# An encoder layer on one core: another order at the entries of gate/up and of down, other slots, some low parts on GpSimd

## The chip, the cores and the metric

One core of one Trainium2 chip runs the kernel. The time is in device microseconds (us). Engines: PE is TensorE, DVE is VectorE, ACT is ScalarE, POOL is GpSimd, SP is SyncE, which only issues DMAs here. SBUF is the on-chip memory, PSUM the accumulators of TensorE, eight banks of 128x512 float32.

## The reference

```python
u = rms_norm(x, norm_mix_g)
proj = einsum('bsd,de->bse', u, w_in)            # q k v | b c h
att  = diff_attention(...) ; conv = bg * short_conv(cg * hv, conv_w)
x = x + einsum('bse,ed->bsd', concat(att, conv), w_out)
z = rms_norm(x, norm_ffn_g)
hid = silu(z @ w_gate) * (z @ w_up)              # 1024 -> 2816
x = x + hid @ w_down
return rms_norm(x, final_g)
```

Everything is float32, the sequence has 2048 rows of 1024. The change concerns the way from the projection with w_out (the rows `x + mixed @ w_out`) through gate/up to the start of down.

## The kernel before, in words

**Three products for one.** TensorE multiplies in a format with fewer bits. Each operand is split: ACT makes the high part (`*_hi`), DVE the low part (`*_lo = raw - hi`), and TensorE makes hi*hi + hi*lo + lo*hi.

**Projection and tiles of z.** 16 tiles of 128 rows (`N_ROWS`, in the order `ORDER`) go one after another: PE projects (`project_tile`, into PSUM banks 0-1 for even and 2-3 for odd tiles, `o_sums`), DVE adds the rows (`add_rows`), ACT squares (`square_rows`), DVE makes the mean, POOL the power -1/2 (`rsqrt_row`), DVE scales to `z_tile` (`norm_rows`), PE turns it (`turn_z`, into banks 4 to 7), ACT evacuates it into `zt` (`evacuate_z`). SP stores the rows (`store_rows`). For each pair of tiles DVE forms four differences `zt_sum` (`sum_z`), and SP stores zt and zt_sum as seven blocks (`store_z`, seven DMAs of 256 KB) into `z_dram`. `evacuate_z` of a pair's first tile waits until the pair before is stored.

**Gate/up as seven products.** The product z @ [gate, up] is made as a 2x2 block product with seven instead of eight block products (k = 0 to 6), for 22 chunks of 128 columns (steps) and for two halves of 1024 rows: 44 steps. Each block product is 4 x 3 matmuls of 128x512. Its operands are the block z_k (`z_slot`, 128x4x512, hi and lo, loaded once in a half) and the weights w_k (`w_slot`, made anew in each step; `sum_weights` forms the sums). Products share four banks (`c_bank`, `BANK_OF`), so in a step product 2 waits for `p_0` (ACT's copy of bank 0), product 5 for `make_u_3`, product 6 for `make_c_22` on DVE. `silu_first`, `hidden` and `silu_second` make the hidden block, which SP stores (`store_hid`).

**Where z blocks come from.** In half 0 blocks 0 to 3 go through `z_stage` (SP loads, ACT's and DVE's `split_z`), blocks 4 to 6 are loaded straight into the place of their low part (`split_placed_z`). In half 1 all seven go through three stages (`load_z_next`): a stage is loaded again once the low part made from it is done. They are made during the last step of half 0 (`later`), each after that step's product k has released its slot.

**Down.** For each of 4 groups of 512 rows, 22 chunks: SP loads 128x512 of the hidden block and 128x1024 of w_down (`load_down`) into one of two slots, ACT and DVE split (`split_down`), PE multiplies into eight banks (`down_chunk`, 24 matmuls). A slot is loaded again once its low parts are done. Ahead of chunk 2 SP issues the y rows and the gain of the end.

**What sets the order.** Every engine runs its instructions in the order of the code, with hand-written semaphores. Only the waits listed in the code hold an instruction up, and everything behind it on that engine with it; SP's DMAs too are issued in one order.

## Time and profile before

| | |
|---|---|
| median of 3 runs (2779.66 to 2782.27) | 2781.87 us |
| the profiled execution: its own time | 2779.97 us |
| its span | 2778.1 us |
| PE busy | 2665.7 us, 96% of the span, 12280 matmuls |
| DVE / ACT / POOL busy | 54% / 37% / 18% |
| granted clock of TensorE over the span | 0.988 |
| lines of gate/up (L1734) on the chain that ended last | 15% |
| lines of down (L1792) on that chain | 17% |

The span is the part of the execution that the profile covers; 1.9 us lie outside it. The profile lists for each group of instructions its busy time and the idle time of its engine just ahead of it, with what ended that. An engine's idle time costs only where the end of the kernel hangs on it. A matmul of 128x512 is shown with 390 ns but one begins every 227 ns; durations of matmuls overlap.

### The profile page before, as it was taken

The page shows a single profiled execution, that of the slowest core. Times are in us where ns is not written, and L with a number is a line of the kernel's source. Part 1 is how long each engine was busy: PE and PEld are TensorE (multiplying, and loading weights), DVE is VectorE, ACT ScalarE, POOL GpSimd, SP SyncE. Part 2 cuts the span into 40 slices and gives each one's busy share as a digit, 9 for nine tenths or more (in the row PEclk, how much of TensorE's full clock was granted, in tenths as well). Part 3 has the DMA queues.
Part 4 walks back from the last instruction along what each step waited for, and adds up shares of the span by engine and source line. Part 5 has one row for each costly group of instructions (what it writes and reads, how often), then busy time and mean ns, then how long its engine had stood idle before and what let it go on. Part 6 is the DMA issues. An engine that isn't in the chain of part 4 may idle for free. (4 is left out here: it accounts for less than half of the span.)

```text
span 2778.1 us, 34594 instructions
## 1 busy us (share of the span) xinstructions
PE 2665.7 (96%) x12280; PEld 2184.4 (79%) x12280; DVE 1511.9 (54%) x2203; ACT 1021.9 (37%) x1429; POOL 501.2 (18%) x343
## 2 busy tenths in 40 slices
PE   7999999979999999989989999989999999999997
PEld 5788888857777777778868888878888878888886
DVE  5311122258878887854466666676666643434343
ACT  5210000047667676742243333343333323323232
POOL 1000000047777777720000000000000000000000
PEclk9999999999999999999989999999999999999999
DMA  5542111223131221047762222252222235556563
GB/s 171 147 124 87 57 38 38 61 64 71 28 75 46 68 57 31 20 157 224 229 219 76 83 91 72 87 174 91 72 87 88 75 120 152 170 175 207 146 203 116
DMA packets 257359, 298.29 MB, mean 107 GB/s; under 512 B 15200, under 2 KB 175456, under 8 KB 257280
## 3 DMA queue, kind: packets, MB, share of 16 engines
q1 hardware_dynamic: 254400, 287.83, 35.1%
q0 software_dynamic: 2304, 8.39, 0.7%
q8 instruction: 46, 0.75, 0.1%
q10 hardware_dynamic: 576, 1.05, 0.1%
q14 instruction: 33, 0.27, 0.0%
HBM read 212.28 MB, written 84.93 MB: 107 GB/s over the span
## 5 line engine op out<-in xcount | busy, mean ns | idle before, releaser
L1734 PE MATMUL banks<-z_hi,w_hi 128*128 128x512 f32 x1204 | 469.9, 390 | 8.4 <-ACT p L947 5.5
L1734 PE MATMUL banks<-z_hi,w_lo 128*128 128x512 f32 x1204 | 469.4, 390 | 0.0
L1734 PE MATMUL banks<-z_lo,w_hi 128*128 128x512 f32 x1204 | 469.3, 390 | 0.0
L1546 PE MATMUL projected<-u_t_hi,w_part_hi 128*128 128x512 f32 (+1 forms) x768 | 300.3, 391 | 5.3 <-DVE u_t_lo L1090 2.6
L1546 PE MATMUL projected<-u_t_lo,w_part_hi 128*128 128x512 f32 (+1 forms) x768 | 299.3, 390 | 0.0
L1546 PE MATMUL projected<-u_t_hi,w_part_lo 128*128 128x512 f32 (+1 forms) x768 | 299.3, 390 | 0.0
L697 POOL TENSOR_TENSOR exp<-exp,exp 128x2048 f32<-128x2048 f32 x64 | 295.6, 4618 | 5.3
L1734 PEld LDWEIGHTS banks<-z_hi,w_hi 128*128 128x128 f32 x1204 | 226.8, 188 | 56.8 <-issue 5.9
L1734 PEld LDWEIGHTS banks<-z_lo,w_hi 128*128 128x128 f32 x1204 | 226.8, 188 | 47.0
L1734 PEld LDWEIGHTS banks<-z_hi,w_lo 128*128 128x128 f32 x1204 | 226.6, 188 | 47.2
L842 ACT ACTIVATE exp<-exp,neg_max 128x2048 f32<-128x2048 f32 x128 | 257.3, 2010 | 15.3 <-DVE neg_max L1228 14.4
L726 POOL TENSOR_TENSOR y_rstd<-y_mean,neg_half 128x1 f32<-128x1 f32 x16 | 8.7, 546 | 1343.4 <-DVE y_mean L1496 1343.4
L943 ACT ACTIVATE w_hi<-w_sum 128x512 fp32r<-128x512 f32 x176 | 111.3, 633 | 319.1 <-PE banks L1734 307.3
L1792 PE MATMUL banks<-down_hi,hid_hi 128*128 128x512 f32 x704 | 217.7, 391 | 3.9 <-DVE down_lo L1484 3.9
L1792 PE MATMUL banks<-down_lo,hid_hi 128*128 128x512 f32 x704 | 217.7, 390 | 0.0
L1792 PE MATMUL banks<-down_hi,hid_lo 128*128 128x512 f32 x704 | 217.4, 390 | 0.0
L852 ACT ACTIVATE a_t_hi<-tile_turned 128x512 fp32r<-128x512 f32 x256 | 148.7, 601 | 158.1 <-PE tile_turned L1622 157.8
L1240 DVE TENSOR_TENSOR a_t_lo<-tile_turned,a_t_hi 128x512 fp32r<-128x512 f32 x256 | 172.1, 687 | 54.3 <-ACT a_t_hi L852 54.2
L1604 PE MATMUL scores<-k_sum,q_part_hi 128*128 128x512 f32 x512 | 179.4, 432 | 18.7 <-DVE half_min L1228 10.3
L1481 DVE TENSOR_TENSOR hid_lo<-hid_raw,hid_hi 128x512 fp32r<-128x512 f32 x88 | 60.9, 693 | 247.6 <-ACT hid_hi L1029 247.6
L1228 DVE CUSTOM_DVE_ANT_0 exp<-scores,window,half_min 128x1024 f32<-128x1024 f32 x128 | 163.9, 1280 | 31.7 <-PE scores L1604 26.1
L1029 ACT ACTIVATE hid_hi<-hid_raw 128x512 fp32r<-128x512 f32 x88 | 55.6, 632 | 324.2 <-PE banks L1792 313.4
(143 smaller groups left out, 4420.9 us busy)
## 6 DMA issues: line engine op xcount, KB each, us to landing
down_raw<-in_w_down SPq DMA_DIRECT2D x88, 512.0 KB, 4.4
gate_raw<-in_w_gate SPq DMA_DIRECT2D x44, 512.0 KB, 4.7
up_raw<-in_w_up SPq DMA_DIRECT2D x44, 512.0 KB, 5.6
hidden_t<-hid_stage SPq DMA_DIRECT2D x88, 256.0 KB, 2.7
hid_raw<-hidden_t SPq DMA_DIRECT2D x88, 256.0 KB, 3.7
w_raw<-in_w_in SPq DMA_DIRECT2D x24, 512.0 KB, 5.3
projected_t<-stage SPq DMA_DIRECT2D x48, 256.0 KB, 2.5
z_stage<-z_blocks SPq DMA_DIRECT2D x11, 1024.0 KB, 5.8
```

What stands on the lines that cost most here:

```text
L697: nc.gpsimd.tensor_tensor(exp_0[:, slot_0], exp_0[:, slot_0], exp_1[:, slot_1], ALU.add).then_inc(mixed_ready, 1)
L842: nc.scalar.activation(rows, rows, ACT.Exp, scale=-1.0, bias=neg_max[:, t % 2, part:part + 1], accum_out=exp_sum[:, part, t % 16:t % 16 + ...
L852: nc.scalar.activation(dst, turned_bank(h, t, index), ACT.Copy).then_inc(group_hi, 1)
L943: nc.scalar.activation(w_slot[k][0][:, :, :], src, ACT.Copy).then_inc(w_hi_ready_2, 1)
L1029: nc.scalar.activation(hid_part[slot][0][:, :], hid_raw[:, slot], ACT.Copy).then_inc(f_hi_ready, 1)
L1228: nc.vector.tensor_tensor_reduce(out=rows[:, half * HALF:(half + 1) * HALF], in0=scores[:, unit % 2], in1=window[:, window_slice(t, half)] ...
L1240: nc.vector.tensor_tensor(parts[1][at], turned_bank(h, t, index), parts[0][at].bitcast(FP32), ALU.subtract).then_inc(group_lo, 1)
L1481: nc.vector.tensor_tensor(hid_part[slot][1][:, :], hid_raw[:, slot], hid_part[slot][0][:, :].bitcast(FP32), ALU.subtract).then_inc(f_lo_re ...
L1546: last = nc.tensor.matmul(projected[:, bank * BANK:(bank + 1) * BANK], w_part[w][:, r, kt], u_t[u][:, kt, rows], start=(kt == 0 and n == 0 ...
L1604: last = nc.tensor.matmul(scores[:, unit % 2, b * BANK:(b + 1) * BANK], q_part[n][:, (t // 4) % 2, part, t % 4 * P:(t % 4 + 1) * P], k_sum ...
L1734: last = nc.tensor.matmul(c_bank[BANK_OF[k]], w_slot[k][w][:, kt], z_slot[k][z][:, kt], start=(kt == 0 and t == 0 and k in (0, 1, 3, 4)), ...
L1792: last = nc.tensor.matmul(y_banks[j][:, c * BANK:(c + 1) * BANK], hid_part[slot][h][:, j * P:(j + 1) * P], down_part[slot][w][:, c * BANK: ...
```

## The change

- The outputs of a step (`up_0`, `silu_0`, `hid_stage`), the weight slots 5 and 6, stage 1 of z and `hid_raw` change places in SBUF. The new place of weight slots 5 and 6 is free when the projection has ended, no longer when the rows have been stored.
- `c_bank` are now banks 0 to 3 (before 0, 1, 4, 5), so that product 3 waits for the last addition of rows instead of an evacuation. `y_banks` follow.
- SP: `store_z` of pair 6 moves behind the loads of z blocks 4 to 6 and the rows of the last tile. The loads for half 1 no longer wait for the stores of the rows, and wait for low parts on their engine.
- ACT: z_hi 3 stands ahead of the square of the last tile; the weights 3 to 6 follow, then z_hi 4, 5 and 6 with the two last evacuations between them.
- DVE: no `sum_z` of pairs 6 and 7, low part of z block 3 ahead of the last mean; the low part of block 5 goes away.
- POOL: makes `sum_z` of pairs 6 and 7 and the low parts of block 5 (half 0) and of blocks 1, 3 and 5 (half 1), with a semaphore of its own (`z_lo_pool`).
- Down: ACT splits chunk 1 ahead of `silu_second`, DVE splits chunk 0 ahead of `make_c_12`.

ScalarE at the entry of gate/up, before (`z_hi_100` is block 3, `z_hi_102`, `_104`, `_106` are blocks 4 to 6, `w_hi_139` to `_145` the weights 3 to 6):

```order
L921 ACTIVATE zt<-banks 128x1024
L914 ACTIVATE z_tile,row_sumsq<-rows 128x1024
L921 ACTIVATE zt<-banks 128x1024
L928 ACTIVATE z_hi_100<-z_stage_147 128x2048
L943 ACTIVATE w_hi_139<-w_sum 128x512
L947 ACTIVATE p_150<-banks 128x512
L943 ACTIVATE w_hi_141<-w_sum 128x512
L921 ACTIVATE zt<-banks 128x1024
L943 ACTIVATE w_hi_143<-up_raw_159 128x512
L943 ACTIVATE w_hi_145<-w_sum 128x512
L932 ACTIVATE z_hi_102<-z_lo_103 128x2048
L932 ACTIVATE z_hi_104<-z_lo_105 128x2048
```

and now:

```order
L965 ACTIVATE zt<-banks 128x1024
L972 ACTIVATE z_hi_100<-z_stage_147 128x2048
L958 ACTIVATE z_tile,row_sumsq<-rows 128x1024
L991 ACTIVATE p_150<-banks 128x512
L987 ACTIVATE w_hi_139<-w_sum 128x512
L987 ACTIVATE w_hi_141<-w_sum 128x512
L987 ACTIVATE w_hi_143<-up_raw_159 128x512
L987 ACTIVATE w_hi_145<-w_sum 128x512
L976 ACTIVATE z_hi_102<-z_lo_103 128x2048
L965 ACTIVATE zt<-banks 128x1024
L976 ACTIVATE z_hi_104<-z_lo_105 128x2048
L965 ACTIVATE zt<-banks 128x1024
```

The last tile's square moved behind z_hi 3, both evacuations (`zt<-banks`) behind the weights and between the placed blocks.

SyncE there, before and now:

```order
L581 DMA z_stage_147<-z_blocks 128x4x512
L533 DMA z_blocks<-zt 128x4x128 x3
L536 DMA z_blocks<-zt_sum 128x4x128 x4
L527 DMA rows_x<-rows 128x1024
L571 DMA z_lo_103<-z_blocks 128x4x512
L571 DMA z_lo_105<-z_blocks 128x4x512
L571 DMA z_lo_107<-z_blocks 128x4x512
L527 DMA rows_x<-rows 128x1024
```

```order
L540 DMA rows_x<-rows 128x1024
L584 DMA z_lo_103<-z_blocks 128x4x512
L584 DMA z_lo_105<-z_blocks 128x4x512
L584 DMA z_lo_107<-z_blocks 128x4x512
L540 DMA rows_x<-rows 128x1024
L546 DMA z_blocks<-zt 128x4x128 x3
L549 DMA z_blocks<-zt_sum 128x4x128 x4
```

The seven stores of a pair moved behind the three loads and the rows.

GpSimd from the last power op of the projection to the change of the half, now (before, the power op was its last instruction there; `z_lo_105` is block 5, `z_lo_97` and `z_lo_101` are blocks 1 and 3 of the second half):

```order
L734 TENSOR_TENSOR row_rstd<-row_mean,neg_half 128x1
L751 TENSOR_TENSOR z_lo_105<-z_lo_105,z_hi_104 128x2048
L741 TENSOR_TENSOR zt_sum<-zt 128x512
L742 TENSOR_TENSOR zt_sum<-zt 128x512
L744 TENSOR_TENSOR zt_sum<-zt,zt_sum 128x512
L746 TENSOR_TENSOR zt_sum<-zt,zt_sum 128x512
L751 TENSOR_TENSOR z_lo_97<-z_stage_148,z_hi_96 128x2048
L751 TENSOR_TENSOR z_lo_101<-z_stage_147,z_hi_100 128x2048
L751 TENSOR_TENSOR z_lo_105<-z_stage_149,z_hi_104 128x2048
```

Four low parts are new on this engine, and eight differences, of which four stand ahead of the power op.

VectorE at the change of the half, before (`z_lo_95` is block 0, `z_lo_97` block 1, `z_lo_99` block 2; `u_151<-banks` is the addition after product 1, `u_152` the one that product 5 waits for) and now:

```order
L1314 TENSOR_TENSOR z_lo_95<-z_stage_147,z_hi_94 128x2048
L1360 TENSOR_TENSOR u_151<-banks,p_150 128x512
L1354 TENSOR_TENSOR w_lo_136<-w_sum,w_hi_135 128x512
L1347 TENSOR_TENSOR w_sum<-gate_raw_157,up_raw_159 128x512
L1349 TENSOR_TENSOR w_sum<-gate_raw_157,w_sum 128x512
L1314 TENSOR_TENSOR z_lo_97<-z_stage_148,z_hi_96 128x2048
L1354 TENSOR_TENSOR w_lo_138<-gate_raw_157,w_hi_137 128x512
L1314 TENSOR_TENSOR z_lo_99<-z_stage_149,z_hi_98 128x2048
L1360 TENSOR_TENSOR u_152<-banks,u_151 128x512
L1354 TENSOR_TENSOR w_lo_140<-w_sum,w_hi_139 128x512
```

```order
L1355 TENSOR_TENSOR z_lo_95<-z_stage_147,z_hi_94 128x2048
L1401 TENSOR_TENSOR u_151<-banks,p_150 128x512
L1395 TENSOR_TENSOR w_lo_136<-w_sum,w_hi_135 128x512
L1388 TENSOR_TENSOR w_sum<-gate_raw_157,up_raw_159 128x512
L1390 TENSOR_TENSOR w_sum<-gate_raw_157,w_sum 128x512
L1395 TENSOR_TENSOR w_lo_138<-gate_raw_157,w_hi_137 128x512
L1355 TENSOR_TENSOR z_lo_99<-z_stage_149,z_hi_98 128x2048
L1401 TENSOR_TENSOR u_152<-banks,u_151 128x512
L1395 TENSOR_TENSOR w_lo_140<-w_sum,w_hi_139 128x512
```

z_lo 1 is gone from between the sums and the weights 2; z_lo 3 and z_lo 5 go likewise further on.

The diff (unchanged lines cut):

```diff
@@ -269,22 +269,22 @@
-        w_at = ((147456, 149504), (204288, 206336), (208384, 194048), (167936, 169984), (172032, 174080), (40960, 43008), (45056, 47104))
+        w_at = ((147456, 149504), (204288, 206336), (208384, 194048), (167936, 169984), (172032, 174080), (196096, 198144), (200192, 202240))
         w_slot = [[at(w_at[k][n], f"w_{'hi' if n == 0 else 'lo'}_{k}", [P, 4, P], F32R) for n in range(2)] for k in range(7)]
-        z_stage = [at(offset, f"z_stage_{i}", [P, 4, BANK]) for i, offset in enumerate((131072, 196096, 73728))]
+        z_stage = [at(offset, f"z_stage_{i}", [P, 4, BANK]) for i, offset in enumerate((131072, 65536, 73728))]
         p_0 = at(32768, "p_0", [P, BANK])
...
         up_1 = at(38912, "up_1", [P, BANK])
-        up_0 = at(65536, "up_0", [P, BANK])
-        silu_0 = at(67584, "silu_0", [P, BANK])
-        hid_stage = at(69632, "hid_stage", [P, 2, BANK])
+        up_0 = at(40960, "up_0", [P, BANK])
+        silu_0 = at(43008, "silu_0", [P, BANK])
+        hid_stage = at(45056, "hid_stage", [P, 2, BANK])
         g_raw = [at(81920, "gate_raw_0", [P, KT, P]), at(139264, "gate_raw_1", [P, KT, P])]
...
         down_raw = at(73728, "down_raw", [P, 2, D])
-        hid_raw = at(196096, "hid_raw", [P, 2, BANK])
+        hid_raw = at(65536, "hid_raw", [P, 2, BANK])
         hid_part = [[at(16384 * s + 2048 * n, f"hid_{'hi' if n == 0 else 'lo'}_{s}", [P, BANK], F32R) for n in range(2)] for s in range(2)]
@@ -303,9 +303,9 @@
         z_turned = [banks[:, 4 + 2 * n:6 + 2 * n].rearrange("p b (k q) -> p (b k) q", q=P) for n in range(2)]
-        c_bank = [banks[:, b] for b in (0, 1, 4, 5)]
+        c_bank = [banks[:, b] for b in range(4)]
         BANK_OF = (0, 1, 0, 2, 3, 2, 3)
-        y_banks = [banks[:, b:b + 2].rearrange("p b n -> p (b n)") for b in (2, 6, 0, 4)]
+        y_banks = [banks[:, b:b + 2].rearrange("p b n -> p (b n)") for b in (4, 6, 0, 2)]
@@ -314,6 +314,19 @@
+        Z_ON_POOL = ((5,), (1, 3, 5))
...
+        def z_count(half, k, on_pool):
...
+            return sum((j in Z_ON_POOL[n]) == on_pool for n in range(half + 1) for j in range(7 if n < half else k + 1))
...
+        def wait_z(engine, half, k):
+            if k in Z_ON_POOL[half]:
+                engine.wait_ge(z_lo_pool, z_count(half, k, True))
+            else:
+                engine.wait_ge(z_lo_ready, z_count(half, k, False))
@@ -328,7 +341,7 @@
         z_loaded = [sem(f"z_loaded_{i}") for i in range(3)]
-        z_hi_ready, z_lo_ready = sem("z_hi_ready"), sem("z_lo_ready")
+        z_hi_ready, z_lo_ready, z_lo_pool = sem("z_hi_ready"), sem("z_lo_ready"), sem("z_lo_pool")
         z_placed = [sem(f"z_placed_{k}") for k in (4, 5, 6)]
@@ -562,7 +575,7 @@
                     load_gate_up(0, 0)
-                if n % 2 == 0 and n >= 2:
+                if n % 2 == 0 and 2 <= n < N_ROWS - 2:
                     store_z(n // 2 - 1)
@@ -570,6 +583,8 @@
                 store_rows(n)
+                if n == N_ROWS - 1:
+                    store_z(N_ROWS // 2 - 2)
                 if n + 2 < N_ROWS:
@@ -577,7 +592,7 @@
                     else:
-                        sp.wait_ge(z_lo_ready, n - 10)
+                        wait_z(sp, 0, n - 11)
                     sp.dma_start(z_stage[0][:, :, :], z_dram[0, n - 10].rearrange("k p t -> p k t")).then_inc(z_loaded[0], 16)
@@ -588,9 +603,11 @@
-                sp.wait_ge(z_lo_ready, 7 + k - 2)
+                if k >= 3:
+                    wait_z(sp, 1, k - 3)
+                elif k == 0:
+                    wait_z(sp, 0, 3)
                 sp.wait_ge(z_stored[1], 16 * 28)
-                sp.wait_ge(rows_stored[k % 2], 16 * (N_ROWS // 2))
                 sp.dma_start(z_stage[k % 3][:, :, :], z_dram[1, k].rearrange("k p t -> p k t")).then_inc(z_loaded[k % 3], 16)
@@ -643,7 +660,8 @@
             sp.wait_ge(hid_stored[1], 16 + 16 * F_CHUNKS)
-            sp.wait_ge(z_lo_ready, 14)
+            wait_z(sp, 1, 5)
+            wait_z(sp, 1, 6)
             load_down(0, 0, 0, False)
@@ -715,8 +733,34 @@
-            for n in range(N_ROWS):
+            def sum_z(pair):
+                pool.wait_ge(zt_ready, 2 * pair + 2)
+                pool.wait_ge(z_stored[(pair - 1) // 4], 16 * 7 * ((pair - 1) % 4 + 1))
+                b11, b21, b12, b22 = zt[:, 0, 0:4], zt[:, 0, 4:8], zt[:, 1, 0:4], zt[:, 1, 4:8]
+                t1, t2, t3, t4 = (zt_sum[:, n] for n in range(4))
+                nc.gpsimd.tensor_tensor(t1, b12, b11, ALU.subtract).then_inc(zt_sum_ready, 1)
+                nc.gpsimd.tensor_tensor(t3, b22, b12, ALU.subtract).then_inc(zt_sum_ready, 1)
+                pool.wait_ge(zt_sum_ready, 4 * pair + 1)
+                nc.gpsimd.tensor_tensor(t2, b22, t1, ALU.subtract).then_inc(zt_sum_ready, 1)
+                pool.wait_ge(zt_sum_ready, 4 * pair + 3)
+                nc.gpsimd.tensor_tensor(t4, b21, t2, ALU.subtract).then_inc(zt_sum_ready, 1)
...
+            def split_z(half, k):
+                pool.wait_ge(z_hi_ready, 7 * half + k + 1)
+                raw = z_stage[k % 3][:, :, :] if half else z_slot[k][1][:, :, :].bitcast(FP32)
+                nc.gpsimd.tensor_tensor(z_slot[k][1][:, :, :], raw, z_slot[k][0][:, :, :].bitcast(FP32), ALU.subtract).then_inc(z_lo_pool, 1)
...
+            for n in range(N_ROWS - 1):
                 rsqrt_row(n)
+            sum_z(N_ROWS // 2 - 2)
+            rsqrt_row(N_ROWS - 1)
+            for k in Z_ON_POOL[0]:
+                split_z(0, k)
+            sum_z(N_ROWS // 2 - 1)
...
+            for k in Z_ON_POOL[1]:
+                split_z(1, k)
@@ -977,10 +1021,14 @@
             for n in range(N_ROWS):
+                if n == N_ROWS - 1:
...
+                    act.wait_ge(o_summed, N_ROWS)
+                    split_z(0, 3, 0, 4)
                 square_rows(n)
...
                     split_m(n + 2)
-                if n >= 1:
+                if 1 <= n < N_ROWS - 1:
                     evacuate_z(n - 1)
@@ -988,26 +1036,20 @@
-            act.wait_ge(o_summed, N_ROWS)
-            split_z(0, 3, 0, 4)
-            split_w(0, 0, 3, True)
             copy_p_0(0)
-            split_w(0, 0, 4, True)
+            for k in range(3, 7):
+                split_w(0, 0, k, True)
+            split_placed_z(4)
+            evacuate_z(N_ROWS - 2)
+            split_placed_z(5)
             evacuate_z(N_ROWS - 1)
+            split_placed_z(6)
...
             act.wait_ge(rows_stored[1], 16 * (N_ROWS // 2))
-            for k in range(5, 7):
-                split_w(0, 0, k, True)
-            split_placed_z(4)
-            split_placed_z(5)
+            silu_first(0)
             split_w(1, 1, 0)
             split_w(1, 1, 1)
-            split_placed_z(6)
...
-            act.wait_ge(z_stored[1], 16 * 28)
-            silu_first(0)
             for k in range(2, 7):
@@ -1038,9 +1080,8 @@
             split_down(0, 0, 0, False)
+            split_down(0, 1, 1, False)
             silu_second(STEPS - 1)
-            act.wait_ge(product_ready, 7 * STEPS)
-            split_down(0, 1, 1, False)
             for group in range(4):
@@ -1427,8 +1468,10 @@
                     dve.wait_ge(ffn_gain_loaded, 16)
+                if n == N_ROWS - 1:
+                    split_z(0, 3, 0)
                 norm_rows(n)
-                if n % 2 == 0 and n >= 2:
+                if n % 2 == 0 and 2 <= n < N_ROWS - 2:
                     sum_z(n // 2 - 1)
@@ -1438,24 +1481,23 @@
                     split_z(0, n - 11, 0)
-            split_z(0, 3, 0)
+            make_u_2(0)
             split_w(0, 0, 3)
-            make_u_2(0)
-            for k in range(4, 7):
-                split_w(0, 0, k)
+            split_w(0, 0, 4)
             split_placed_z(4)
-            sum_z(N_ROWS // 2 - 1)
+            split_w(0, 0, 5)
             make_u_3(0)
-            split_placed_z(5)
+            split_w(0, 0, 6)
+            split_placed_z(6)
+            make_c_22(0)
             sum_weights(1, 1, 0)
             split_w(1, 1, 0)
-            make_c_22(0)
             split_w(1, 1, 1)
-            split_placed_z(6)
             sum_weights(1, 1, 1)
...
-            dve.wait_ge(z_stored[1], 16 * 28)
+            dve.wait_ge(rows_stored[0], 16 * (N_ROWS // 2))
+            dve.wait_ge(rows_stored[1], 16 * (N_ROWS // 2))
             make_c_21(0)
@@ -1468,7 +1510,7 @@
                 gate_up_step(2 * pair + 2, 0)
-            gate_up_step(F_CHUNKS - 1, 1, lambda k: split_z(1, k, k % 3))
+            gate_up_step(F_CHUNKS - 1, 1, lambda k: None if k in Z_ON_POOL[1] else split_z(1, k, k % 3))
             with dve.Fori(F_CHUNKS // 2, F_CHUNKS - 1) as pair:
@@ -1506,9 +1548,9 @@
             hidden(STEPS - 1, 0)
+            split_down(0, 0, 0)
             make_c_12(STEPS - 1)
             hidden(STEPS - 1, 1)
-            split_down(0, 0, 0)
             split_down(0, 1, 1)
@@ -1713,7 +1755,7 @@
                 if fresh is not None:
-                    pe.wait_ge(z_lo_ready, 7 * fresh + k + 1)
+                    wait_z(pe, fresh, k)
@@ -1738,7 +1780,7 @@
                 pe.wait_ge(w_lo_ready_2, k + 1)
-                pe.wait_ge(z_lo_ready, k + 1)
+                wait_z(pe, 0, k)
                 if k == 2:
@@ -1766,7 +1808,7 @@
             first_product(2)
-            pe.wait_ge(zt_ready, N_ROWS - 1)
+            pe.wait_ge(rows_added, N_ROWS)
             for k in range(3, 7):
```

## Rows read from the trace of the kernel before

**Rows 1.** timeline of TensorE: start, us, engine, line, operation [idle before <- releaser].

```profile
1416.73 0.77 PE L1750 MATMUL banks<-z_hi,w_hi 128*128 128x512 f32 x1 [2.57 <-ACT p L947]
...
1430.47 0.77 PE L1750 MATMUL banks<-z_hi,w_hi 128*128 128x512 f32 x1 [5.27 <-DVE z_lo L1320]
...
1441.96 0.47 PE L1750 MATMUL banks<-z_hi,w_hi 128*128 128x512 f32 x1 [2.99 <-issue]
...
1446.31 0.47 PE L1734 MATMUL banks<-z_hi,w_hi 128*128 128x512 f32 x1
...
1843.43 0.50 PE L1734 MATMUL banks<-z_hi,w_hi 128*128 128x512 f32 x1 [2.47 <-DVE u L1360]
...
1860.82 0.77 PE L1734 MATMUL banks<-z_hi,w_hi 128*128 128x512 f32 x1 [5.51 <-ACT p L947]
...
2281.02 1.22 PE L1792 MATMUL banks<-down_hi,hid_hi 128*128 128x512 f32 x2 [3.91 <-DVE down_lo L1484]
```

**Rows 2.** windows, TensorE alone: stretch, us, busy (instructions), granted clock, DMA share, GB/s.

```profile
1600.00:1800.00 200.00, 200.00 (x884) 1.00 0.28 85
1416.73:1425.04 8.31, 8.31 (x24) 0.65 1.05 351
1860.82:1866.08 5.26, 5.26 (x12) 0.50 0.15 55
```

**Rows 3.** timeline of DVE and of GpSimd in the first stage.

```profile
33.09 1.27 DVE L1084 SCALAR_TENSOR_TENSOR u_tile<-x_tile,rstd,mix_gain 128x1024 f32<-128x1024 f32 x1
33.26 1.52 POOL L682 TENSOR_TENSOR rstd<-mean_eps,neg_half 128x1 f32<-128x1 f32 x1 [0.69 <-DVE mean_eps L1077]
...
40.58 0.69 DVE L1096 TENSOR_TENSOR stage<-projected,stage 128x512 fp32r<-128x512 f32 x1
40.73 0.55 POOL L682 TENSOR_TENSOR rstd<-mean_eps,neg_half 128x1 f32<-128x1 f32 x1 [5.95 <-DVE mean_eps L1077]
```

**Rows 4.** single lines: durations in ns, least/median/most, first and last start, shapes.

```profile
L697 POOL TENSOR_TENSOR exp<-exp,exp x64: 4507/4627/4651, 588.6 to 1194.4; 128x2048 f32<-128x2048 f32 x64
...
L1314 DVE TENSOR_TENSOR z_lo<-z_stage,z_hi x3: 2287/2292/2292, 1384.4 to 1415.6; 128x2048 fp32r<-128x2048 f32 x3
```

**Rows 5.** DMA issues in windows at 1401.6, 1411.7 and 1418.0: KB, us to landing.

```profile
z_stage<-z_blocks SPq DMA_DIRECT2D x1, 1024.0 KB, 5.5
...
z_lo<-z_blocks SPq DMA_DIRECT2D x1, 1024.0 KB, 11.4
...
z_blocks<-zt SPq DMA_DIRECT2D x1, 256.0 KB, 10.0
```

**Rows 6.** timeline of SP and ScalarE at the entry of gate/up.

```profile
1409.86 2.57 SPq L571 DMA_DIRECT2D z_lo<-z_blocks  x3
...
1412.76 1.03 ACT L921 ACTIVATE zt<-banks 128x1024 f32<-128x1024 f32 x1 [1.88 <-DMA z_blocks<-zt_sum]
```

**Rows 7.** timeline of ScalarE, DVE and SP at the change of the half.

```profile
1833.46 1.91 ACT L928 ACTIVATE z_hi<-z_stage 128x2048 fp32r<-128x2048 f32 x1
...
1835.28 0.68 DVE L1360 TENSOR_TENSOR u<-banks,p 128x512 f32<-128x512 f32 x1
...
1850.33 0.69 DVE L1386 TENSOR_TENSOR hid_stage<-up,silu 128x512 f32<-128x512 f32 x1
...
1851.51 0.37 SPq L594 DMA_DIRECT2D z_stage<-z_blocks  x1
...
1857.77 1.91 ACT L928 ACTIVATE z_hi<-z_stage 128x2048 fp32r<-128x2048 f32 x1 [7.16 <-DMA z_stage<-z_blocks]
```

**Rows 8.** timeline of SP, ScalarE and TensorE at the entry of down, chunk 2.

```profile
2282.49 0.41 SPq L640 DMA_DIRECT2D hid_raw<-hidden_t  x1
...
2290.73 0.63 ACT L1029 ACTIVATE hid_hi<-hid_raw 128x512 fp32r<-128x512 f32 x1 [10.75 <-DMA hid_raw<-hidden_t]
2291.94 1.06 ACT L1031 ACTIVATE down_hi<-down_raw 128x1024 fp32r<-128x1024 f32 x1 [0.58 <-DMA down_raw<-in_w_down]
...
2294.41 0.64 PE L1792 MATMUL banks<-down_hi,hid_hi 128*128 128x512 f32 x2
```

## The prediction

> **What bounds the kernel now.** Read the waits of TensorE first, because TensorE is busy for 96% of the span and the steady loops leave it no idle time: what a change outside its instruction count can give is only where it stands still or runs at its low clock. The waits that belong to the lines of this change are four kinds, and the timeline puts them in three places [rows 1]:
>
> - *Entry of gate/up, 1412 to 1446.3 us.* Products 2 to 6 of step 0 stand behind an evacuation (2.57), the low part of z block 4 (5.27) and that of block 6 (2.99).
> - *Change of the half, 1831 to 1866 us.* Product 5 waits 2.47, product 2 of the next step 5.51.
> - *Entry of down, 2277 to 2294 us.* The first chunk waits 3.91.
>
> Together about 23 us. Each wait also costs clock. In the steady loop 884 matmuls take 200 us, 0.226 each, so a product of 12 takes 2.7; after the 5.51 us wait the granted clock was 0.50 (the 1.2 GHz level) and 12 matmuls took 5.26 us; after the 2.57 us wait 24 of them took 8.31 us instead of 5.4 [rows 2]. So an idle time of 2.6 us or more brings some 2.6 us with it, one of 2.47 brought none. At the entry of gate/up three such stretches bring about 7 us. In all some 35 us of 2780 could go, if nothing else set these places. So the question at each place is what comes last once the named wait is gone.
>
> **Two things the sum needs.** *DVE and GpSimd exclude each other.* GpSimd's tiny power op takes 0.55 us, also beside a DVE instruction that reads PSUM (started 40.73, beside the one of 40.58). The one started at 33.26 took 1.52: a DVE instruction with two SBUF inputs had begun at 33.09 and ended at 34.36 [rows 3]. Three of the 16 power ops of that line met such a DVE instruction, and exactly these three took 1.5 us. I take it that the exclusion holds in the other direction too; the rows don't show that, since in attention, where GpSimd works long, DVE's instructions all read PSUM. GpSimd's add of 128x2048 took 4.62 us, DVE's low part of the same shape 2.29 [rows 4]; a quarter of the first, 1.2 us, is my estimate for 128x512.
> The Trainium skill, page "SBUF — State Buffer", section "SBUF: two separate sides", says the same in both directions: GpSimd and a DVE instruction with two SBUF inputs share a port pair as "an exclusive lock, not a bandwidth split". By it the loser stands for the whole instruction. It speaks against this change: moving work to GpSimd then frees next to nothing on DVE.
> *The DMA queue lands in order at some 350 GB/s.* The third 1 MB block, issued at 1411.7, landed after 11.4 us; a 256 KB store issued at 1418.0 behind it took 10.0 us; the fourth z_stage block, issued at 1401.6, landed at 1407.1 [rows 5]. Between 1416.7 and 1425.0 the queue moved 351 GB/s [rows 2].
>
> **Part 1, entry of gate/up.** Removed: the late issue of the three blocks (before from 1409.86 on, behind the stores of pair 6 [rows 6]; now at 1406.0, when the last projection ends), ScalarE's wait for the row stores ahead of the weights 5 and 6, DVE's 2 x 4 sums (4 x 0.6 us each), one low part on DVE. The last tile's chain: its addition on DVE comes at 1406.1 instead of 1408.5. But z_hi 3 now stands ahead of its square on ScalarE (1407.2 to 1409.1), then the low part z_lo 3 on DVE ahead of the mean; with GpSimd's four sums between, z_lo 3 runs 1409.7 to 1412.0, the last sum to 1413.2, the power op to 1413.8, z_tile to 1415.1. The turn comes 2 us later than before, product 2 starts at about 1416, product 4 ends at about 1427: before, only products 2 and 3 were done by 1425.
> What comes last next: ScalarE evacuates tile 14 into zt only once pair 6 is stored. Before, that wait ended at 1412.76 [rows 6]. Now pair 6 is issued behind everything: left in the queue at 1407.1 are the rows of tile 14 (0.52 MB), the three blocks (3.15), the rows of tile 15 (0.52), pair 6 (1.84), 6.03 MB at 351 GB/s = 17.2 us, so it lands at 1424.5. And in ScalarE's order z_hi 5 stands behind that evacuation: evacuation to 1426, z_hi 5 to 1427.9, evacuation of tile 15 to 1428.8, z_hi 6 to 1430.7. GpSimd makes z_lo 5 in 4.6 us, to 1432.6. Product 5 starts there, 5.6 us after product 4 ended, at the low clock (5.3 us), product 6 follows and ends at 1440.7. DVE's z_lo 6 waits for GpSimd and is done by 1434.9, the sum for product 6 by 1435.5, the first weights of step 1 by 1440.5 even if GpSimd's second group of sums comes between each pair: in time. Step 1 began at 1446.3 [rows 1]: **-5.5 us**, from -10 (pair 6 lands at 1420) to -1 (a full queue that holds up SP).
>
> **Part 2, change of the half.** Low parts 1, 3 and 5 go from DVE to GpSimd; the loads' issues keep their order. Before: z_hi 1 starts at 1833.46 and ends at 1835.3, DVE adds from PSUM at 1835.28 [rows 7]. Now GpSimd begins z_lo 1 at 1835.4, while DVE does that addition, and holds until 1840.0. DVE's next instruction (the low weights, two SBUF inputs) ends at 1840.7 instead of 1836.6; two sums, low weights and z_lo 2 to 1844.7; the addition that product 5 needs ends at 1845.4, and TensorE has waited 4.4 us instead of 2.5, with the low clock behind it. GpSimd takes z_lo 3 from 1844.8 to 1849.4: DVE's low weights 3 wait for it and with them the addition for product 6 (1850.7; product 5 ends then too). z_lo 4 on DVE ends at 1853.5, z_hi 5 is ready at 1853.2 (product 5 must have ended), GpSimd gets in with z_lo 5 while DVE adds from PSUM, to 1858.2. The hidden block, before at 1850.33, comes to 1858.2; SP's load of z block 6 stands behind its store (before 1851.51), is issued at 1859.5 instead, lands 6 us later, z_hi 6 ends at 1867.3 instead of 1859.7 [rows 7]. Behind it on ScalarE is p_0, for which TensorE waited 5.51 us. **+7 us**; if DVE gets its hidden block in before GpSimd +4; from +3 to +9 under exclusion. Where both run side by side: z_lo 4 still waits for its load (lands at 1845.4), the hidden block comes at 1850.1, the load at 1851.2: -0.3 us, at best -2.
>
> **Part 3, entry of down.** Chunk 0's low parts now go ahead of the last combination. DVE ends them at 2277.6, TensorE starts at 2277.8 instead of 2281.0, without the wait and at full clock, so chunks 0 and 1 (48 matmuls) are done at 2288.7 instead of 2294.4. But chunk 2 was just in time: its data are issued at 2282.49 behind 2.6 MB of y rows and gain, ScalarE's hid_hi waited for them until 2290.73 and down_hi until 2291.94, DVE's low part (1.2 us) filled the rest, TensorE went on at 2294.41 [rows 8]. None of these issues moves forward; SP's second store of the hidden block is 0.4 us later. So TensorE now waits 6 us at 2288.7 and starts chunk 2 at 2294.8, at the low clock (2.5 us more for the first 12 matmuls). In the kernel before, that price lay inside the time in which chunk 2 was awaited anyway. **+2.9 us**, from 0 (clock stays) to +3.5.
>
> Sum: -5.5 + 7.0 + 2.9 = **+4.4 us** on the profiled execution's 2779.97 (span 2778.1, 1.9 outside it), which is 1.9 below the median 2781.87; against the median that is 2786.3. The rest (banks, slots) changes no count and no size: 12280 matmuls before and now.
>
> **The rivals.**
> *Side by side.* GpSimd doesn't hold up DVE. For: no row shows GpSimd delaying DVE, and 4.6 us adds ran in attention without DVE's instructions there growing longer. Against: the three long power ops [rows 3]. Then -5.5 - 0.3 + 2.9 = -2.9: 2779.0.
> *The waits go as named.* Pair 6 lands early, chunk 2's data come with the chunk, no low clock: part 1 -10, part 2 -1, part 3 -3, -14 in all, 2768. For: the store of pair 6 needs only the time of its own 1.84 MB where the queue ahead is short. Against: 4 MB stand ahead of it now, and the rows of chunk 2 leave no slack [rows 5, 8].
> *Slower beyond doubt.* Exclusion as in part 2, where z_lo 5 gets ahead of the hidden block (+7.6), and pair 6 landing 4 us later, which takes part 1 to -1.5: -1.5 + 7.6 + 2.9 = +9, 2791. It decides as soon as pair 6 lands after 1428.
> *The change does less than it says:* GpSimd's sums come so late that store and load of the next weights stall step 1; a loss of 2 to 4 us more in part 1, inside the case above.
>
> **How the numbers follow.** Exclusion with part 1 near -5.5: 0.52, 2786.3 (own range 2781 to 2789). Exclusion with a late queue: 0.18, 2791. Side by side: 0.18, 2779. Waits go as named: 0.12, 2768. A measurement can tell about 0.2%, 5.6 us: faster is under 2776.3, slower over 2787.4. Faster: all of the last, a third of side by side, a little of the first: 0.20. Slower: most of the late-queue case, a third of the first: 0.33. The range 2773 to 2792 leaves out the last rival and the tails.
>
> **What would show it.** Part 1: ScalarE's zt of tile 14 waits for a store until about 1424, TensorE idles before product 5 and not before product 4. Part 2: DVE instructions that took 0.69 are shown with 2 to 5 us beside z_lo on GpSimd, z block 6 is issued near 1859. Part 3: TensorE starts down at 2278 (on the clock of before) and stands 6 us before chunk 2. I am wrong if DVE's durations stay at 0.69 beside GpSimd, if pair 6 lands by 1420, or if chunk 2's hid_raw lands before 2289.

## The result and the profile after

| | median | range, runs |
|---|---|---|
| kernel before | 2778.41 us | 2775.04 to 2782.27, 18 |
| changed kernel | 2782.48 us | 2780.08 to 2786.30, 18 |

The ratio is 1.0019 with a 95% interval of 1.0012 to 1.0025: 3 to 7 us slower, a small loss but clear of no change. Forecast were +4.4 us over the kernel before, or 2786.3 us by the 2781.87 us that the kernel before had then; its median of 18 runs is 3.5 us lower, and the changed kernel's 2782.48 us lies 3.8 under the forecast time. The profiled execution has a span of 2782.4 us, against 2778.1 before; the counts of matmuls are equal.

*A measure that is free of the front.* What lies ahead of gate/up varies by some us between executions, for every kernel here: in the thirteen profiles the 15th addition of rows on DVE starts between 1398.0 and 1404.7 us. So the stages are measured from the start of that addition. Its row in the trace after, then TensorE's first product line of the steps from 1 on (how many, shortest/mean/longest in ns, first to last start):

```profile
1399.50 1.22 DVE L1344 TENSOR_TENSOR rows<-banks,rows 128x1024 f32<-128x1024 f32 x1
L1776 PE MATMUL banks<-z_hi,w_hi x1204: 389/389/792, 1438.0 to 2277.5; 128*128 128x512 f32 x172
```

and the same two of before:

```profile
1401.50 1.22 DVE L1303 TENSOR_TENSOR rows<-banks,rows 128x1024 f32<-128x1024 f32 x1
L1734 PE MATMUL banks<-z_hi,w_hi x1204: 389/389/765, 1446.3 to 2276.3; 128*128 128x512 f32 x172
```

Three lengths follow for each kernel: from that addition to step 1 (44.8 us before, 38.5 after), from there to the last gate/up matmul (830.0, 839.5), and from that to the end of the span (501.8, 504.9). These lengths don't repeat to a tenth: among kernels with the same code in a stage (table below) they differ by 1.1 us to step 1 (37.6 to 38.7; before and e11 by 2.2), by 1.7 in the middle (837.8 to 839.5) and by 1.7 in the last (503.9 to 505.6). Of the 9.5 us that the middle one grew, 2.3 lie ahead of the change of the half (DVE's addition `u<-banks,p` comes 389.0 us after step 1 began in before, 391.3 in after), so 7.2 lie at it. The three parts of the forecast are therefore: entry of gate/up -6.3 + 2.3 = **-4.0** (forecast -5.5), change of the half **+7.2** (+7.0), entry of down **+3.1** (+2.9). The span's difference of 4.3 has 2.0 us of a shorter front in it: 1399.50 against 1401.50.

TensorE's timeline after, its first matmul behind each long wait (start, length, instruction, in brackets the idle time ahead and what ended it). The rows that answer are [rows 1]:

```profile
1412.94 1.13 PE L1751 MATMUL banks<-identity,z_tile 128*128 128x128 f32 x8 [2.26 <-DVE z_tile L1350]
1430.83 0.77 PE L1792 MATMUL banks<-z_hi,w_hi 128*128 128x512 f32 x1 [7.03 <-issue]
1445.69 0.50 PE L1776 MATMUL banks<-z_hi,w_hi 128*128 128x512 f32 x1 [1.92 <-ACT p L991]
...
1839.28 0.79 PE L1776 MATMUL banks<-z_hi,w_hi 128*128 128x512 f32 x1 [4.32 <-DVE u L1401]
1861.85 0.76 PE L1776 MATMUL banks<-z_hi,w_hi 128*128 128x512 f32 x1 [9.15 <-ACT p L991]
...
2278.92 0.74 PE L1834 MATMUL banks<-down_hi,hid_hi 128*128 128x512 f32 x2 [0.58 <-DVE down_lo L1526]
2296.20 1.22 PE L1834 MATMUL banks<-down_hi,hid_hi 128*128 128x512 f32 x2 [6.07 <-DVE down_lo L1526]
```

Three waits of the entry became one long one (product 5) and a new small one in step 1; both waits at the change of the half grew (2.47 to 4.32, 5.51 to 9.15); the 3.91 us of chunk 0 became 6.07 us ahead of chunk 2. The four long ones were followed by low clock, the one of 1.92 by the full one (granted 1.00 from 1445.69 to 1451.10). The windows behind the four (length, PE busy and count, granted clock, DMA share, GB/s):

```profile
1430.83:1436.30 5.47, 5.47 (x17) 0.68 0.16 48
1839.28:1845.00 5.72, 5.72 (x15) 0.59 0.59 183
1861.85:1867.20 5.35, 5.35 (x13) 0.50 0.15 53
2296.20:2301.60 5.40, 5.39 (x13) 0.52 0.72 210
```

*Change of the half: GpSimd, then DVE beside it.*

```profile
1829.44 4.63 POOL L751 TENSOR_TENSOR z_lo<-z_stage,z_hi 128x2048 fp32r<-128x2048 f32 x1 [390.31 <-ACT z_hi L972]
1837.84 5.21 POOL L751 TENSOR_TENSOR z_lo<-z_stage,z_hi 128x2048 fp32r<-128x2048 f32 x1 [3.77 <-ACT z_hi L972]
1847.01 4.61 POOL L751 TENSOR_TENSOR z_lo<-z_stage,z_hi 128x2048 fp32r<-128x2048 f32 x1 [3.96 <-ACT z_hi L972]
```

```profile
1829.29 0.69 DVE L1401 TENSOR_TENSOR u<-banks,p 128x512 f32<-128x512 f32 x1
1829.89 4.73 DVE L1395 TENSOR_TENSOR w_lo<-w_sum,w_hi 128x512 fp32r<-128x512 f32 x1
1834.54 0.68 DVE L1388 TENSOR_TENSOR w_sum<-gate_raw,up_raw 128x512 f32<-128x512 f32 x1
...
1836.35 2.28 DVE L1355 TENSOR_TENSOR z_lo<-z_stage,z_hi 128x2048 fp32r<-128x2048 f32 x1
...
1839.15 4.45 DVE L1395 TENSOR_TENSOR w_lo<-w_sum,w_hi 128x512 fp32r<-128x512 f32 x1
...
1847.69 4.47 DVE L1427 TENSOR_TENSOR hid_stage<-up,silu 128x512 f32<-128x512 f32 x1
```

For each instruction of GpSimd one of DVE stands with 4.5 to 4.7 us instead of 0.69, and ends some 0.55 us behind GpSimd's end (1829.44 + 4.63 = 1834.07, and DVE's 1829.89 + 4.73 = 1834.62): it began its work only then. The other direction is in GpSimd's second row: 5.21 us instead of 4.6, because DVE's z_lo 2 of 1836.35 ran until 1838.6. The addition from PSUM at 1829.29 ran with its usual 0.69 while GpSimd began. The last of them is the hidden block; behind its store stands SP's load of z block 6, and behind that ScalarE:

```profile
1852.63 0.39 SPq L611 DMA_DIRECT2D z_stage<-z_blocks  x1
```

```profile
1858.80 1.91 ACT L972 ACTIVATE z_hi<-z_stage 128x2048 fp32r<-128x2048 f32 x1 [10.86 <-DMA z_stage<-z_blocks]
```

### The profile page after: what moved, and what is told of

Same layout as the page of the kernel before. It is cut to its first block and busy times, and to the rows that moved or that the text cites. A ratio compares the mean times of both kernels' runs of the same rounds, so it can differ in the third digit from the quotient of the medians.

```text
span 2782.4 us, 34593 instructions
## 1 busy us (share of the span) xinstructions
PE 2662.5 (96%) x12280; PEld 2182.5 (78%) x12280; DVE 1514.2 (54%) x2191; ACT 1020.6 (37%) x1429; POOL 536.5 (19%) x355
```

## The experiments

Each kernel ran in five rounds with the kernel before beside it; the kernel before had 2778.53, 2777.84 and 2777.50 us in the three groups (e1, e2, e4, e5; e3, e6, e7, e8; e9 to e11). Lengths in the table are the three of above, from the profiled execution, in us. They are those of one execution: their sums and the medians differ from each other by up to 4 us (most in e5 and e11, whose profiled executions were the shortest of their runs). So a median decides what an edit is worth, and the lengths say where; a difference under 2 us between two lengths is not told from none. Why executions of one kernel differ so is open; one part that shows is the clock behind a wait (last section).

| kernel | median | ratio to before, 95% | to step 1 | step 1 to last gate/up | to the end |
|---|---|---|---|---|---|
| before | | | 44.8 | 830.0 | 501.8 |
| changed | 2782.48 | 1.0019, 1.0012 to 1.0025 | 38.5 | 839.5 | 504.9 |
| e1_half_on_vector | 2775.57 | 0.9989, 0.9980 to 0.9998 | 37.6 | 831.0 | 503.9 |
| e2_down_undone | 2780.06 | 1.0008, 0.9999 to 1.0017 | 38.4 | 837.8 | 501.7 |
| e4_y_rows_later | 2774.89 | 0.9988, 0.9979 to 0.9997 | 37.8 | 838.0 | 496.4 |
| e5_placed_first | 2776.96 | 0.9995, 0.9986 to 1.0004 | 31.0 | 838.1 | 504.1 |
| e3_block6_ahead | 2769.20 | 0.9969, 0.9958 to 0.9980 | 37.9 | 824.6 | 505.6 |
| e8_y_rows_alone | 2779.12 | 1.0008, 0.9999 to 1.0017 | 38.6 | 838.1 | 501.1 |
| e7_halves | 2779.39 | 1.0005, 0.9996 to 1.0014 | 38.7 | 836.3 | 504.5 |
| e6_all | 2754.73 | 0.9919, 0.9905 to 0.9932 | 30.9 | 824.7 | 496.7 |
| e9_block5_on_vector | 2755.36 | 0.9917, 0.9903 to 0.9931 | 33.6 | 823.5 | 496.5 |
| e10_sums_on_vector | 2755.05 | 0.9919, 0.9905 to 0.9933 | 30.8 | 823.8 | 496.4 |
| e11_before_two_places | 2766.30 | 0.9959, 0.9945 to 0.9973 | 42.6 | 822.4 | 496.1 |

### The change of the half

**e1_half_on_vector**, the changed kernel without GpSimd's low parts of the second half:

```diff
-        Z_ON_POOL = ((5,), (1, 3, 5))
+        Z_ON_POOL = ((5,), ())
```

> One part undone: the low parts 1, 3 and 5 of the second half are made by VectorE again, GpSimd keeps block 5 of the first half and the two groups of sums. Theory (GpSimd and VectorE with two SBUF inputs exclude each other, and this is what made the change of the half 7.2 us longer): the stretch from step 21 to step 23 is as in the kernel before, no VectorE instruction of 128x512 there takes over 0.7 us, z block 6 is issued some 5 us earlier; in all 7 us less than the changed kernel, -1 us against the kernel before. Rival (the stretch is longer because the stage was moved or because the loads wait for other semaphores): stays at +4 us against the kernel before.

The middle length went from 839.5 back to 831.0, the median down by 6.9 us. The moved stage and the loads' other semaphores, the rival's causes, are still in this kernel. So GpSimd's low parts alone made the loss at this place.

**e7_halves**, the changed kernel with each of GpSimd's low parts there as two instructions:

```diff
-                nc.gpsimd.tensor_tensor(z_slot[k][1][:, :, :], raw, z_slot[k][0][:, :, :].bitcast(FP32), ALU.subtract).then_inc(z_lo_pool, 1)
+                    nc.gpsimd.tensor_tensor(z_slot[k][1][:, 0:2], raw[:, 0:2], z_slot[k][0][:, 0:2].bitcast(FP32), ALU.subtract)
+                    nc.gpsimd.tensor_tensor(z_slot[k][1][:, 2:4], raw[:, 2:4], z_slot[k][0][:, 2:4].bitcast(FP32), ALU.subtract).then_inc(z_lo_pool, 1)
```

> The changed kernel with each of GpSimd's three low parts of the second half as two instructions of 128x1024 (4.6 us becomes 2.3 + 2.3). Theory (DVE waits for the GpSimd instruction that runs, and gets its turn between two): no DVE instruction there is longer than about 3.0 us (2.3 + 0.7) instead of 4.7, the hidden block comes earlier, and the change of the half costs 1 to 4 us less: about 2779 to 2781. Rival (GpSimd keeps the port as long as it has a next instruction ready): DVE's longest stay at 4.7 us and the time at 2782.5.

GpSimd's timeline and DVE's beside it, at the first of the three low parts:

```profile
1831.84 2.41 POOL L752 TENSOR_TENSOR z_lo<-z_stage,z_hi 128x1024 fp32r<-128x1024 f32 x1 [390.30 <-ACT z_hi L976]
1834.21 2.84 POOL L753 TENSOR_TENSOR z_lo<-z_stage,z_hi 128x1024 fp32r<-128x1024 f32 x1
```

```profile
1832.28 2.52 DVE L1399 TENSOR_TENSOR w_lo<-w_sum,w_hi 128x512 fp32r<-128x512 f32 x1
1834.72 2.88 DVE L1392 TENSOR_TENSOR w_sum<-gate_raw,up_raw 128x512 f32<-128x512 f32 x1
```

The two take turns, one instruction each: DVE's low weights ended 0.55 us behind GpSimd's first half (1834.80 and 1834.25), and GpSimd's second half shows 0.4 us more than its first. DVE's longest 128x512 instruction at the change of the half was 2.88 us, the kernel 3 us faster. So DVE waits for the instruction that runs, and the rival, that GpSimd keeps its place while it has a next one, fell.

**e3_block6_ahead**, e1 with the load of z block 6 ahead of the store of the hidden block:

```diff
-            for k in range(3, 6):
+            for k in range(3, 7):
                 load_z_next(k)
             store_hid(0, F_CHUNKS - 1, F_CHUNKS - 1, 0)
-            load_z_next(6)
```

> The low parts of the second half are all on DVE again, as in e1_half_on_vector, and z block 6 is loaded ahead of the store of the hidden block. Theory: at the change of the half TensorE's wait for p_0 (4.8 us in e1, 5.5 in before) is there only because that load stands on SP behind a store that waits for DVE's hidden block; with the load issued as soon as z_lo 3 is made, that wait goes and the low clock behind it (2.6 us) too, so some 7 us less than e1 and 10 less than before: about 2768. Rival: the slot of z block 3 comes free no earlier than the store's block, or the last product waits for ScalarE's copies anyway: then within 2 us of e1, 2774 to 2776.

It gave 2769.20, 6.4 us under e1, as the theory said: the wait for `p` at the change of the half is gone (its two, 6.7 us, became one of 1.9 in step 1). TensorE's waits there, by line and releaser (total, times, longest), of e1 and then e3:

```profile
PE banks L1776 <- ACT p L991: 6.7, 2, 4.8
```

```profile
PE banks L1775 <- ACT p L990: 1.9, 1, 1.9
```

The 5.51 us of [rows 1] stood with all the low parts on DVE too (4.8 us in e1): one load stood behind a store that waited for DVE. Who makes the low parts set only how long the wait was (9.15 us in the changed kernel).

### The entry of down

**e2_down_undone** puts the low parts of chunk 0 behind the last combination again, and ScalarE's chunk 1 behind the last product:

```diff
-            split_down(0, 0, 0)
             make_c_12(STEPS - 1)
             hidden(STEPS - 1, 1)
+            split_down(0, 0, 0)
```

> One part undone: both splits at the entry of down stand again where they stood before. Theory (TensorE's earlier start only makes it wait for chunk 2, at the low clock): chunk 2 starts at once after chunk 1 as in the kernel before, 3 us less than the changed kernel, about +1 us against the kernel before (-4.0 of part 1, +7.2 of part 2 in the traces, less the 2 us by which that profiled run was ahead already). Rival (an earlier start is a gain, the 3.1 us come from a later second store of the hidden block): 3 us more than the changed kernel, +7 us.

The last length is 501.7, before's 501.8, and the median 2.4 us under the changed kernel's (forecast 3): part 3's +3.1 is the early split.

**e4_y_rows_later**, the changed kernel with chunks 2 and 3 loaded ahead of the y rows and the gain, which DVE awaits at its first use:

```diff
             sp.wait_ge(product_ready, 7 * STEPS)
+            load_down(0, 2, 0)
+            load_down(0, 3, 1)
             load_y_rows(0)
...
-            with sp.Fori(1, F_CHUNKS // 2) as pair:
+            with sp.Fori(2, F_CHUNKS // 2) as pair:
```

> The changed kernel, with the loads of down's chunks 2 and 3 issued ahead of the y rows and the gain, and VectorE waiting for the gain only at its first use. Theory (chunk 2 is late because 2.6 MB stand ahead of it in the queue): chunk 2's hid_raw lands by 2286, TensorE has no wait and no low clock there; 9.4 us less than the changed kernel (3.1 + 3.9 + 2.4), -5 us against the kernel before. Rival (chunk 2 is late because SP is held by the store of the hidden block): at most 2 us less than the changed kernel.

The last length fell to 496.4, 8.5 under the changed kernel and 5.4 under before; the median fell by 7.6, somewhat less than the 9.4 of the theory. ScalarE had chunk 2's data at 2286, as the theory said, though SP issued that load right behind the store of the hidden block; so the rival fell:

```profile
2285.98 0.63 ACT L1073 ACTIVATE hid_hi<-hid_raw 128x512 fp32r<-128x512 f32 x1 [5.61 <-DMA hid_raw<-hidden_t]
```

**e8_y_rows_alone** has the same load order and e2's late split:

> Chunks 2 and 3 of down are loaded ahead of the y rows as in e4_y_rows_later, but chunk 0 and 1 are split as late as in the kernel before. Theory: TensorE waits 3.9 us for chunk 0 as in before, runs its first 12 matmuls at the low clock, and chunk 2 (in time already in before, by a hair) brings nothing more: from the last gate/up matmul to the end 500 to 502 us, as before (501.8) and against 496.4 in e4, the time 3 to 4 us below the changed kernel. That is, the early split pays only together with the early load. Rival: the y rows' place alone is what counts: 496 to 498 us.

501.1, and a median 3.4 us under the changed kernel's, as forecast: the load order alone is worth nothing that can be told (0.7 us over before, where such lengths repeat to 1.7), the early split alone costs 3.1, both together gain 5.4. Chunk 2's arrival and chunk 0's start are two constraints at one place; in before the first came just in time for what the second allowed.

### The entry of gate/up

**e5_placed_first**, the changed kernel with ScalarE's z_hi 5 and 6 and its first silu ahead of both evacuations:

```diff
-            split_placed_z(4)
-            evacuate_z(N_ROWS - 2)
-            split_placed_z(5)
-            evacuate_z(N_ROWS - 1)
-            split_placed_z(6)
+            for k in (4, 5, 6):
+                split_placed_z(k)
...
             silu_first(0)
+            evacuate_z(N_ROWS - 2)
+            evacuate_z(N_ROWS - 1)
```

> The changed kernel, with ScalarE's high parts of blocks 4, 5 and 6 and the first silu ahead of the evacuations of tiles 14 and 15, which wait for the store of pair 6. Theory (this wait, 10.34 us until 1423.3 in the profile of the changed kernel, sets product 5 at the entry of gate/up): z_hi 5 starts once its block has landed, some 8 us earlier, TensorE's wait of 7.03 us and the low clock behind it go; 8 to 10 us less than the changed kernel, -5 us against the kernel before. Rival (the blocks land no earlier than the evacuation, or GpSimd's sums and low part of block 5 come last): 0 to 3 us less.

Step 1 began 7.5 us earlier (31.0 against 38.5), the 7.03 us wait gone. So it was the order on ScalarE, not the arrival of z block 5, that made it. The median fell by 5.5 us only, between the 8 to 10 of the theory and the rival's 0 to 3; the three lengths together say 9.7, but they are those of the shortest of this kernel's runs. What the order is worth is therefore known as 5 to 10 us; a wait of 1.17 us for low weights, new ahead of step 1, is inside the 31.0. In the changed kernel the evacuation waited for pair 6, with z_hi 5 behind it:

```profile
1423.32 1.02 ACT L965 ACTIVATE zt<-banks 128x1024 f32<-128x1024 f32 x1 [10.34 <-DMA z_blocks<-zt_sum]
1424.25 1.90 ACT L976 ACTIVATE z_hi<-z_lo 128x2048 fp32r<-128x2048 f32 x1
```

**e6_all**: e1, e3, e4 and e5 together.

> Four edits together: low parts of the second half on DVE, z block 6 loaded ahead of the store, chunks 2 and 3 of down ahead of the y rows with the gain waited for late, and ScalarE's z_hi 5 and 6 and first silu ahead of both evacuations. Theory: the places are apart in time, so the savings against the changed kernel add up: 7 (e1) + 7 (block 6) + 7.6 (e4) + 5.5 (e5) = 27, about 2755. Rival: what is saved at one place is waited for at the next (the store of the hidden block, the late sums of the last pair and the loads behind them): 5 to 15 us less of it, 2760 to 2770.

2754.73, 23 us under before and 28 under the changed kernel, about the sum of the four that the theory gave (27; their medians add up to 26.4): the places are far enough apart not to disturb each other. It is the fastest kernel of this study, level with the next two. TensorE's waits between 1380 and 2320 us in it, all above 1 us:

```profile
PE banks L1752 <- DVE z_tile L1350: 3.2, 2, 2.2
PE banks L1777 <- DVE u L1401: 2.5, 1, 2.5
PE banks L1777 <- ACT p L992: 1.9, 1, 1.9
PE banks L1777 <- DVE w_lo L1395: 1.2, 1, 1.2
```

**e9_block5_on_vector** takes from e6 GpSimd's last low part, **e10_sums_on_vector** from e9 also its sums of the last pair:

```diff
-        Z_ON_POOL = ((5,), ())
+        Z_ON_POOL = ((), ())
...
             make_u_3(0)
+            split_placed_z(5)
             split_w(0, 0, 6)
             split_placed_z(6)
             make_c_22(0)
+            sum_z(N_ROWS // 2 - 1)
```

(the last line only in e10, with GpSimd's call removed).

> e6_all with the low part of z block 5 of the first half on DVE as well (2.3 us there), so that GpSimd keeps only the sums of the last two pairs. Theory (exclusion: what GpSimd takes over costs DVE its full length): in e6 DVE's low weights beside GpSimd's z_lo 5 take 5.1 us instead of 0.7, that is 4.4 us lost for 2.3 us of work taken over; so DVE is some 2 us further, TensorE's wait of 1.2 us for low weights in step 1 goes, and the time is 1 to 3 us under e6_all (2752 to 2754). Rival: the entry of gate/up is bound by z blocks and not by DVE, so DVE's 2.3 us more come to TensorE's path: 1 to 2 us over e6_all.

> e9_block5_on_vector with the four sums of the last pair on DVE as well (4 x 0.7 us in a row, behind its third combination). Theory: in e6 DVE and GpSimd took turns during these sums, which made four DVE instructions 3.6 us longer in all; in a row on DVE they cost 2.8. So DVE is 0 to 1 us further, the wait for p_0 in step 1 (1.9 us) shrinks at most by that: 0 to -1.5 us against e9. Rival: the sums on GpSimd are what TensorE's 1.9 us wait comes from, and all of it goes with them: -2 to -4 us.

Neither moved the time: 2755.36 and 2755.05 against 2754.73. For e9 the theory missed: the 5.10 us low weights beside GpSimd's z_lo 5 went back to 0.68, but DVE's own z_lo 5 came late in its order, behind an addition that waited for TensorE, the z_lo 6 behind it took 3.39 us instead of 2.28 beside GpSimd's sums, and product 6 then waited 1.55 us. The wait for low weights at the start of step 1, which was to go, is 1.38 us (e6: 1.19). Step 1 began 2.7 us later than in e6, and from there to the last gate/up matmul 1.2 came back. For e10 DVE's four sums took 0.68 or 0.69 each, and the wait for p_0 in step 1 is 1.08 where e6 has 1.9 and e9 0.83: it didn't go with the sums. The median is 0.3 under e9's, within the theory's 0 to -1.5 and outside the rival's -2 to -4; the lengths of the two profiles say 2.6, which is why the medians have to decide. What GpSimd took over of block 5 and of the last pair is thus worth nothing that these runs can tell, in either direction; pair 6's sums stayed on it in every run of the changed kernel.

**e11_before_two_places**: the kernel before with e3's and e4's edits and the early split alone.

> The kernel before with only these edits: z block 6 loaded ahead of the store of the hidden block, chunks 2 and 3 of down loaded ahead of the y rows, the gain waited for at its first use, and the changed kernel's early low parts of chunk 0. Nothing of the changed entry of gate/up. Theory: the 5.5 us wait at the change of the half and the 3.9 us wait at the entry of down go with the low clock behind the first: -5 to -7 and -5.4, so 2765 to 2768. Rival: these two places depend on the changed slots or on the low parts of the changed kernel: no better than 2772.

2766.30, 11.2 us under before, with 822.4 and 496.1 (e6: 824.7 and 496.7). So of e6's 23 us some 11 need nothing of the change. The other 12 are the entry of gate/up (44.8 us, in e11 42.6, to 30.9): there the slots, banks, moved stores and the last tile's chain pay together, once ScalarE's order doesn't take them back. Which of them pays is not shown: no run takes one of them alone, and none gives the kernel before another order on ScalarE only.

## Why the prediction was right, point by point

**Part 1, entry: -5.5 forecast, -4.0 measured.** The chain held nearly word for word. On the clock of before (the trace after is 2.0 us ahead there), pair 6 was to land at 1424.5; the wait for it ended at 1423.32 + 2.0 = 1425.3. (The recorded 1424.5 is 0.2 more than its own sum, 1407.1 + 17.2.) Product 5 was to start at 1432.6 and did at 1432.8; its wait was longer than forecast (7.03 against 5.6) only because product 4 had ended 1.2 us earlier. Step 1 was to begin at 1440.7 and did at 1440.0: products 5 and 6 took 7.2 us where the forecast had 8.1, since the clock behind the wait was granted at 0.68 and not at 0.50. So up to there the gain was 6.3. The term that was put at nothing is what follows: the forecast ended with the first weights of step 1, which were to be in time even with GpSimd's sums between. They were, for product 0. But further on in step 1 TensorE waited for p_0, and DVE, which stands ahead of it, had been slowed by GpSimd: z_lo 6 took 3.99 us instead of 2.28, and two sums and two low weights 1.17 to 1.78 instead of 0.69:

```profile
1433.99 1.73 POOL L742 TENSOR_TENSOR zt_sum<-zt 128x512 f32<-128x512 f32 x1
1435.69 1.75 POOL L744 TENSOR_TENSOR zt_sum<-zt,zt_sum 128x512 f32<-128x512 f32 x1
```

```profile
1434.61 1.67 DVE L1386 TENSOR_TENSOR w_sum<-w_sum,gate_raw 128x512 f32<-128x512 f32 x1
1436.20 1.78 DVE L1395 TENSOR_TENSOR w_lo<-gate_raw,w_hi 128x512 fp32r<-128x512 f32 x1
```

DVE worked without a pause from 1428.89 up to the addition at 1443.81, for which ScalarE waited (`u`, 1444.52), and p_0 stands behind that: 1.92 us of TensorE. How much of it is GpSimd's doing is not settled: with neither block 5 nor the last pair on it the wait is 1.08 us (e10), with the sums on GpSimd 0.83 (e9), with the low part of block 5 too 1.9 (e6). The wait is 1.9 of the 2.3 us given back; the 0.4 left is not taken apart.

**Part 2, change of the half: +7.0 forecast, +7.2 measured.** The exclusion in the direction that no row of before showed is there, with its full length. The forecast wait of 4.4 us for product 5 was 4.32. The trace after is 6.0 us ahead of before at this place (DVE's addition at 1829.29 against 1835.28), so GpSimd's z_lo 5 ended at 1857.6 on the clock of before (forecast 1858.2), the hidden block behind it at 1858.2, and z block 6 was issued at 1858.6 (forecast 1859.5). ScalarE's z_hi 6 ended at 1866.7 (forecast 1867.3), and the first matmul behind p_0 started at 1867.8 instead of 1860.82, 7.0 us later. The forecast's own times would give 7.6 (1867.3 against 1859.7), the number that its rival uses; the 7.0 in its sum is rounded down without a reason given. The Trainium skill, page "SBUF — State Buffer", section "SBUF: two separate sides", calls the shared port "an exclusive lock, not a bandwidth split"; the traces agree, in both directions (4.73 against 0.69 us on DVE, 5.21 against 4.6 on GpSimd), and e7 adds that the lock changes hands between two instructions.

**Part 3, entry of down: +2.9 forecast, +3.1 measured.** TensorE was to start down without a wait and waited 0.58 us; it was to stand 6 us ahead of chunk 2 and stood 6.07, since ScalarE had its data only then:

```profile
2292.42 0.63 ACT L1071 ACTIVATE hid_hi<-hid_raw 128x512 fp32r<-128x512 f32 x1 [12.29 <-DMA hid_raw<-hidden_t]
```

and the clock was at the lower level behind it (0.52). e2, e4 and e8 show the cause from three sides.

**The rivals.** *Side by side* fell with DVE's 4.73 us. *The waits go as named* fell with pair 6 at 1423.3 and chunk 2 at 2292.4. *Slower beyond doubt* needed pair 6 after 1428. *The change does less than it says* was the nearest: step 1 did lose 2.3 us where it had 2 to 4, though by a wait for p_0 and not by a late store or load, and GpSimd's share in it is not settled.

The parts add up to 6.3 us (-4.0 + 7.2 + 3.1) against the forecast 4.4; the 1.9 us are nearly all part 1's (-4.0, against -5.5), which is known to some 2 us. The profiled spans differ by 4.3 only because the front was 2.0 us shorter. The medians differ by 4.1, and the ratio's interval of 3 to 7 us holds both numbers. That 4.1 lies so near the forecast 4.4 is in part luck, and so are the tenths in which parts 2 and 3 agree, since lengths repeat to 1 or 2 us only. What is confirmed is the sign and the cause of each part.

One reading that the forecast used doesn't hold: that an idle time of 2.6 us or more brings some 2.6 us of low clock and one of 2.47 none. The same 2.47 us wait was followed by the full clock in some executions and by a lower mean in others, and 3.91 us cost less in e2 and e8 than in before (last section). The forecast's terms survive because the changed kernel's waits of 4.3 us and more were all followed by low clock, at 0.50 to 0.68.

## What to carry to other kernels

Before work is given to GpSimd to relieve DVE, count DVE's instructions beside it that read two SBUF operands: each GpSimd instruction of 4.6 us stopped one of them for some 4 us, to take 2.3 us off DVE, and taking work back from GpSimd never cost time that could be told (e1, e9, e10). And when a wait is to be removed, look for the load that stands in the queue behind something unrelated: three reorderings of queues (a load ahead of a store, two chunks ahead of rows that are needed much later, a conversion ahead of an evacuation) made some 20 of the 28 us between the changed kernel and e6, where moving arithmetic made a loss. Where two constraints are met within a us of each other, as the end of chunk 1 and the data of chunk 2 were in the kernel before, only moving both pays.
